# Embedding products computed between the routing steps, value projection by K halves, and the last two key blocks of the stick attention summed ahead

## The reference

```
# first block: two-level routing, then the experts
y = expert(hid)                      # hid = silu(x @ w_gate[e]) * (x @ w_up[e]); y = hid @ w_down[e]
# second block
u_x, u_g, q, k, v, g_lru, g_att = split(rmsnorm(x) @ w_in)
log_1m = where(causal, log_sigmoid(-z), 0)            # z = q k^T / 8, causal: key < query
suffix = cumsum(log_1m over keys, reversed) - log_1m
att    = where(causal, exp(log_sigmoid(z) + suffix), 0);   y_att = att @ v
...
x = x + sigmoid(rmsnorm(x) @ w_ple_gate) * (p @ w_ple)       # p: 512 x 256, w_ple: 256 x 1024
out = rmsnorm(x)
```

## Time and profile before

| | |
|---|---|
| median of 3 runs | 1800.84 us (1800.48 to 1802.74) |
| profiled execution | 1802.86 us, its span 1800.0 us |
| PE busy | 1711.8 us, 95% of the span |
| DVE, ACT, POOL busy | 696.6, 605.8, 567.0 us |
| mean granted clock of PE | 0.979 |
| stages of the span | routing 293 to 315, experts to 803, projections to 1042, stick attention to 1225, the rest to 1800 us |

### The profile page before, as it was taken

The page is one execution under the profiler, slowest core; times in us unless marked ns, Lnnn a source line. Parts: engine busy times, 40 slices in busy tenths (PEclk is TensorE's granted clock), DMA queues, the critical chain, the costliest instruction groups (busy, mean ns, idle before and its releaser), DMA issues.

```text
span 1800.0 us, 20351 instructions
## 1 busy us (share of the span) xinstructions
PE 1711.8 (95%) x8350; PEld 1195.8 (66%) x8350; DVE 696.6 (39%) x1060; ACT 605.8 (34%) x787; POOL 567.0 (32%) x263
## 2 busy tenths in 40 slices
PE   7989796999999999989999999999999999999995
PEld 5667574444444443447788977777777888888882
DVE  6564645233433333358541022223244322222325
ACT  5565444111000110025641255555233423232331
POOL 3232134222022201023434334443443444444440
PEclk9989998999999999999999999999999999999997
DMA  5121172699999999972221201112232222223101
GB/s 207 56 74 48 36 294 95 247 420 421 421 421 421 421 421 421 421 285 94 94 94 47 94 1 48 48 48 94 94 141 94 94 94 94 100 91 124 60 36 47
DMA packets 75068, 308.56 MB, mean 171 GB/s; under 512 B 3008, under 2 KB 4448, under 8 KB 50272
## 3 DMA queue, kind: packets, MB, share of 16 engines
q1 hardware_dynamic: 74704, 306.18, 43.6%
q0 software_dynamic: 272, 1.05, 0.2%
HBM read 305.12 MB, written 2.10 MB: 171 GB/s over the span
## 4 chain that ended last, share of the span: by engine, by line
PE 86%; DVE 7%; ACT 3%; issue 2%; POOL 1%; DMA 0%; DVEq 0%; SPq 0%; ACTq 0%
PE ps L857 42%; PE ps L1189 12%; PE ps L899 8%; PE ps L1213 6%; PE ps L1143 4%; PE ps L855 3%; PE ps L1336 2%; PE ps L1158 1%; ACT sb_slot L1403 1%; PE ps L1159 1%; PE ps L1321 1%; PE ps L1357 1%; PE ps L1306 1%; DVE sb_xT L2211 1%; ACT sb_F L1403 1%
## 5 line engine op out<-in xcount | busy, mean ns | idle before, releaser
L797 POOL TENSOR_TENSOR sb_w_parts<-sb_slot,sb_w_parts 128x2048 fp32r<-128x2048 f32 x59 | 274.9, 4660 | 381.6 <-ACT sb_w_parts L1403 381.6
L857 PE MATMUL ps<-sb_h_high,sb_w_parts 128*128 128x512 f32 x1120 | 269.4, 392 | 2.5 <-POOL sb_w_parts L797 2.5
L857 PEld LDWEIGHTS ps<-sb_h_high,sb_w_parts 128*128 128x128 f32 x1120 | 209.7, 188 | 51.0 <-POOL sb_w_parts L797 3.7
L1403 ACT ACTIVATE sb_w_parts<-sb_slot 128x2048 fp32r<-128x2048 f32 x59 | 112.7, 1912 | 186.7 <-PE ps L857 186.7
L1189 PE MATMUL ps<-sb_slot,sb_hT 128*64 128x512 f32 x768 | 171.1, 594 | 0.0
L857 PE MATMUL ps<-sb_hidden_high,sb_w_parts 128*128 128x512 f32 x704 | 165.2, 389 | 1.9 <-ACT sb_hidden_high L1403 1.9
L857 PEld LDWEIGHTS ps<-sb_hidden_high,sb_w_parts 128*128 128x128 f32 x704 | 132.1, 188 | 29.7 <-ACT sb_hidden_high L1403 2.3
L761 POOL TENSOR_TENSOR sb_tile_parts<-sb_slot,sb_tile_parts 128x1024 fp32r<-128x1024 f32 x32 | 79.7, 2492 | 202.5 <-ACT sb_tile_parts L1403 202.5
L857 PE MATMUL ps<-sb_h_low,sb_w_parts 128*128 128x512 f32 x560 | 138.0, 389 | 0.0
L1189 PEld LDWEIGHTS ps<-sb_slot,sb_hT 128*64 128x64 f32 x768 | 53.6, 137 | 106.2 <-issue 106.2
L857 PEld LDWEIGHTS ps<-sb_h_low,sb_w_parts 128*128 128x128 f32 x560 | 105.1, 188 | 21.8
(11 more groups left out here) (313 smaller groups left out, 2651.7 us busy)
## 6 DMA issues: line engine op xcount, KB each, us to landing
sb_slot<-w_up SPq DMA_DIRECT2D x24, 2048.0 KB, 15.5
sb_slot<-w_gate SPq DMA_DIRECT2D x24, 2048.0 KB, 15.4
sb_slot<-w_down SPq DMA_DIRECT2D x21, 2048.0 KB, 16.2
sb_slot<-w_in SPq DMA_DIRECT2D x14, 2048.0 KB, 7.9
sb_R<-w_down SPq DMA_DIRECT2D x11, 2048.0 KB, 16.0
sb_slot<-tiles SPq DMA_DIRECT2D x32, 512.0 KB, 3.4
sb_R<-w_gate SPq DMA_DIRECT2D x8, 2048.0 KB, 15.2
sb_R<-w_up SPq DMA_DIRECT2D x8, 2048.0 KB, 15.9
```

Source lines behind the costliest of these rows:

```text
L797: nc.gpsimd.tensor_tensor(low, raw_part(g), high.bitcast(F32), ALU.subtract).then_inc(w_low, 1)
L857: ins = nc.tensor.matmul(o, w[:, k, at:at + P], h[:, k, :], start=first, stop=last)
L1403: return nc.scalar.activation(dst, src, f, **kw)
```

## The change

1. `p @ w_ple` moves. Its operands (1.5 MB) are loaded in SP's list where chunk 6 was, into slot 2. PE makes `ple` 0 to 2 after the last `turn_h` and `ple` 3 to 7 after `rank`. ACT copies each result to a free piece of slot 2 or `hT`, SP stores the eight pieces (256 KB each) to a DRAM buffer, waits for all of them, and only then loads chunk 6. ACT waits for the same stores before the first expert's SiLU. SP reads the 2 MB back during the MLP.
2. The end. After each `pg` block a step `embed`: DVE multiplies the PSUM bank by `rstd`, ACT takes the sigmoid in the bank, DVE multiplies by `ple` in the bank and adds to x; ACT squares. The last sum of squares is two fp32 matmuls, one of `acc` with seven blocks and one of the eighth square, without DVE's last addition.
3. `v2` by K halves: an item holds 4 of the 8 K blocks and 512 columns. `vh` accumulates the first half in four banks, `v2` the second; 8 jobs, 192 matmuls of 512 columns in all.
4. Stick attention: DVE makes `Ltail` (key block 2, its second half with key block 3 added) and its high part, and signals `tail_done`; POOL waits for that instead of `sp_done` and makes one more low part. PE sums key blocks 2 and 3 for the query sums 0 and 1 together from `Ltail`; only two fp32 matmuls a head are left.

The job numbers shift: eight more before `ux`, eight fewer in `v2`, eight fewer at the end.

```diff
+    for n in range(3):
+        job("ple", n)
     step("route")
     job("rank")
+    for n in range(3, KD):
+        job("ple", n)
     step("place")
...
+            if base == "pg" and n:
+                for m in (0, 1) if n == 1 else (n,):
+                    if n > 1:
+                        step("embed", m)
+                    else:
+                        held.append(m)
...
     elif base == "v2":
-        ITEMS += [(base, (2 * n + h) * TT, TT) for h in range(2)]
+        ITEMS += [("vh", n * TT, TT), ("v2", n * TT, TT)]
...
-            chunk_load(6)
+            load(pT2, a["pT"].rearrange("(k p) n -> p k n", p=P), ld["p"])
+            for k in range(2):
+                load(w_ple[:, :, k, :], a["w_ple_2"][0, k * P:k * P + P, :].rearrange("p (n c) -> p n c", c=P), ld["p"])
             sp.wait_ge(w1_low, len(TILES1))
             chunk_load(1)
             finished(sp, ("tile", "out", KD - 1))
             chunk_load(0)
+            for n in range(KD):
+                taken(sp, ("ple", n))
+                load(ple_rows[n], ple_out[n], stored)
+            sp.wait_ge(stored, 16 * KD)
+            chunk_load(6)
...
-                            pool.wait_ge(sp_done, h + 1)
+                            pool.wait_ge(tail_done, h + 1)
...
+                            ins = nc.gpsimd.tensor_tensor(Ltail_low[h % 2], Ltail[h % 2], Ltail_high[h % 2].bitcast(F32), ALU.subtract)
...
+                if norm == 5:
+                    pe.wait_ge(acc_done, 7 * SQUARED.index(norm) + 6)
+                    nc.tensor.matmul(ps_[:, 7, :], C("ones"), acc, start=True, stop=False)
+                    pe.wait_ge(squared, 8 * SQUARED.index(norm) + KD)
+                    nc.tensor.matmul(ps_[:, 7, :], C("ones"), sq, start=False, stop=True).then_inc(summed, 1)
+                    return
...
                     def suffix_high(h):
                         pe.wait_ge(sp_done, h + 1)
-                        sums(h, tri_r, ones_r, Lhigh, (0, 1, 2))
-                        sums(h, C("negtri"), C("negones"), Lb, (3,))
+                        suffix(h, Lhigh)
+                        c, w_ = SEG[3]
+                        last = Lb[h % 2][:, c:c + w_]
+                        summed_keys(h, 3, 0, P, C("negtri"), last)
+                        summed_keys(h, 2, P, P, C("negones"), last)
+                        pe.wait_ge(tail_done, h + 1)
+                        for jt in range(2):
+                            summed_keys(h, jt, (2 - jt) * P, 2 * P, ones_r, Ltail_high[h % 2])
...
+                elif kind == "embed":
+                    n = arg[0]
+                    job = ("proj", "pg", n)
+                    finished(dve, job)
+                    v.tensor_tensor(bank(job), bank(job), rstd, ALU.mult).then_inc(pg_in, 1)
+                    if n:
+                        add_square(5, n - 1)
+                    else:
+                        dve.wait_ge(ld["p"], 64)
+                    dve.wait_ge(pg_done, n + 1)
+                    link(v.tensor_tensor(bank(job), bank(job), ple[:, n, :], ALU.mult))
+                    frees(v.tensor_tensor(xT[:, n, :], bank(job), xT[:, n, :], ALU.add), job)
+                    taken(dve, job)
+                    dve.sem_inc(x_new, 1)
...
+                        (c2, _), (c3, _) = SEG[2:4]
+                        v.tensor_copy(Ltail[h % 2][:, 0:P], Lb[h % 2][:, c2:c2 + P])
+                        link(v.tensor_tensor(Ltail[h % 2][:, P:2 * P], Lb[h % 2][:, c2 + P:c2 + 2 * P], Lb[h % 2][:, c3:c3 + P], ALU.add))
+                        v.tensor_copy(Ltail_high[h % 2], Ltail[h % 2]).then_inc(tail_done, 1)
```

More of the change, by code:

```diff
@@ L212, in plan @@
         weights_ahead(g)
+        if (base, first) == ("pg", 2):
+            for m in held:
+                step("embed", m)
         if base in ("ux", "ug") and first + (KD if base == "ug" else 0) in (6, 12):
@@ L249, in plan @@
                 step("feed", 5, n - 3 * KD)
-    for n in range(KD):
-        job("proj", "ple", n)
-        step("square", 5, n)
+            if base == "pg" and n:
+                for m in (0, 1) if n == 1 else (n,):
+                    if n > 1:
+                        step("embed", m)
+                    else:
+                        held.append(m)
     step("norm", 5)
@@ L310, in build @@
         xT_ = sb("xT", KD * S)
-        F = sb("F", 1024)
+        with ExitStack() as third:
+            F = third.enter_context(nc.sbuf_tensor("sb_F", [P, 1024], F32))
+        F_parts = sb("F_parts", 1024, F32R)
         cst = sb("cst", NCONST)
@@ L572, in weight_parts @@
             kind, i = buffer_of[g]
+            if ITEMS[g][0] in ("vh", "v2"):
+                return [view(WP, PAN * part + PAN // 2 * i, KD // 2, 512) for part in range(2)]
             return (WH[i], WL[i]) if kind == "whole" else tile_parts[i]
@@ L1126, in _, with ple_taken @@
                     x_bank, odd_bank, even_bank = (0, 1, 7, 2), (7, 0, 1, 4), (7, 0, 1, 2)
+                    def ple_taken(b):
+                        for n in range(KD):
+                            if J["ple", n] % JB == b:
+                                taken(pe, ("ple", n))
                     def gather(m, q):
@@ L1502, in _ @@
                     norm, n = arg
-                    if norm == 5:
-                        act.wait_ge(x_new, n + 1)
-                    else:
-                        taken(act, ("tile", "out", n))
-                        fn(hT[:, n, :], xT[:, n, :], ACT.Copy, scale=G("ffn_norm_g", n)).then_inc(xg_ready, 1)
+                    taken(act, ("tile", "out", n))
+                    fn(hT[:, n, :], xT[:, n, :], ACT.Copy, scale=G("ffn_norm_g", n)).then_inc(xg_ready, 1)
                     square(norm, n)
@@ L1557, in _ @@
                     job = st
-                    o = None if name in ("bl", "ba", "out2", "dn", "ple", "ux", "ug", "q2", "k2", "gl", "ga", "up", "pg") else bank(job)
+                    o = None if name in ("vh", "bl", "ba", "out2", "dn", "ux", "ug", "q2", "k2", "gl", "ga", "up", "pg") else bank(job)
                     if o is not None:
@@ L1576, in _ @@
                         fn(HC[c % 2][0][:, n % KD, :], relu[:, n % 2, :], ACT.Copy).then_inc(hid_high, 1)
-                    elif name == "pg":
-                        taken(act, job)
-                        fn(pgs[:, n, :], pgs[:, n, :], ACT.Sigmoid).then_inc(pg_done, 1)
+                elif kind == "embed":
+                    n = arg[0]
+                    job = ("proj", "pg", n)
+                    act.wait_ge(pg_in, n + 1)
+                    fn(bank(job), bank(job), ACT.Sigmoid).then_inc(pg_done, 1)
+                    act.wait_ge(x_new, n + 1)
+                    square(5, n)
                 elif kind == "soft":
@@ L1665, in _ @@
                     frees(fn(htok[:, t, cols], bank(st), ACT.Copy, scale=row_rstd[:, t:t + 1]), st)
+                elif kind == "ple":
+                    finished(act, st)
+                    frees(fn(ple_out[arg[0]], bank(st), ACT.Copy), st)
                 elif kind == "route":
@@ L1995, in _ @@
                                         ALU.subtract).then_inc(hid_low, 1)
-                    elif name == "ple":
-                        dve.wait_ge(pg_done, n + 1)
-                        finished(dve, st)
-                        if n:
-                            dve.wait_ge(x_new, n)
-                        frees(v.tensor_tensor(prod["ple"], bank(st), pgs[:, n, :], ALU.mult), st)
-                        taken(dve, st)
-                        v.tensor_tensor(xT[:, n, :], xT[:, n, :], prod["ple"], ALU.add).then_inc(x_new, 1)
                 elif kind == "headsum":
```

131 lines of the change are left out of this document (76 added, 55 removed).

## The result

The changed kernel takes 1773.14 us (median; 1772.05 to 1774.92) against 1801.61 us for the kernel before, timed beside it: ratio 0.9845, 95% interval 0.9833 to 0.9858. The forecast was 1774.0 us, within 1768.5 to 1781.5. The profiled execution took 1772.83 us with a span of 1771.0, 29.0 us less than the span before.

What follows compares the result with a forecast made beforehand. PE, busy 95% of the span, was taken as the bound, other engines counting only where PE waits. Terms -19.9 - 2.3 - 2.5 - 2.1 = -26.8 us from the 1800.84 median gave 1774.0 us, range 1768.5 to 1781.5.

Steps and rivals of the forecast that it cites:

- The end, -19.9: Behind the last gate product only block 7's round, square and table load remain, so the root starts 19.9 us earlier.
- the cover I named: At the end, even a half-clock second sum would end at 1767.7, before the table load allows the root at 1767.9.
- Routing, -2.3: Embedding products in PE's routing waits keep the clock up; the first gather falls from 10.18 to 7.85 us.
- rival b: Small parts pay in full and one clock dip elsewhere is gone: -4.4 - 1.7 on top, 1768 us; chance 0.13.
- v2, -2.5: Value projection: 192 matmuls of 512 columns take 43.6 us instead of 46.08 for 384 of 256.
- Stick, -2.1: Stick attention: seven pair periods each 0.65 us shorter, -4.5, against +2.4 in the first pair; bounds -6.5 to +3.
- The first pair: First pair of heads in stick attention: +1.6 us from later low parts and +0.8 from the clock, together +2.4.
- the 0.8 us that I gave to the clock: First pair of heads: with more PE idle time the already low clock may fall sooner, +0.8 us.
- Rival d: Expert stream starts late; each us chunk 6 is issued after about 324.7 costs one us: 1801 and more; chance 0.03.

Runs made afterwards that it cites:

- improved: Changed kernel with six unread matmuls in three PE idle times, POOL's first stick subtraction started earlier and the first pair's first fill low pass moved: 1772.08 us.
- gap_filled: Kernel before with only 16 unread matmuls added in routing, 6 ahead of the rank product and 10 behind it: 1799.45 us.
- stick_alone: Kernel before with only the stick attention part of the change: 1799.20 us against 1801.65 us.
- late_chunk: Changed kernel with one more wait in SP's list, so expert chunk 6 is issued only when the first chunk has been used: 1772.03 us.
- after_again: The changed kernel unchanged, timed once more: 1774.41 us.
- v2_alone: Kernel before with only the value projection by K halves: 1801.41 us against 1801.65 us.
- longer_rounds: Changed kernel with one more DVE multiplication by 1.0 in each round of embed: 1776.91 us (two executions).

## Why the prediction was right

- **The end, -19.9: -20.0.** Rounds of 2.92 us (I had 3.0), one block left. One term was wrong: the second sum, which I put at half of 1.02, is a whole fp32 product, 1.13 us. The clock was full, as I had said. It ended at 1758.76, 0.1 us ahead of the table load's end, so it cost nothing, but the cover I named was nearly used up; in `improved`, where it ran at a low clock (1.77 us), it was not enough.
- **Routing, -2.3: -2.27**, by the mechanism named (`gap_filled`), and 1.7 us more for the dip at 787, which I had only in rival b. Chunk 6 was issued at 315.34 (I said about 317), the next one near 328.5.
- **v2, -2.5: -2.34**; the passes themselves fell from 46.08 to 43.53 us, and 0.2 us came back in a longer eviction of 512 columns ahead of the scores.
- **Stick, -2.1.** The first pair lost 2.31 (+2.4) and the period fell by 0.75 to 0.77 us (0.65). The three DVE operations took 0.22, 0.28 and 0.29, POOL's 0.73, as priced. I had POOL 0.3 us late and PE waiting for it before the odd head's low sums; that wait isn't there. POOL ends at 1116.58 and PE's low sums begin at 1116.63 without a break, so the two tie, and the period fell by 0.1 us more than I wrote. `stick_alone` has the same: 20.76 and 21.38 us. Without the dip in the second pair of before the stage is 3.0 us shorter, against 2.1. The first pair was right in size, but for a reason of which I had only the half. The 1.5 us of added operations were priced; the 0.8 us that I gave to the clock were not lost to it (its dip there cost nothing), but to DVE and POOL in each other's way, 0.45 + 0.52 us on DVE's side. That 2.4 came out is luck to that extent.
- **Rival d** had a wrong rule, that each us of late stream costs one us. In `late_chunk` it cost 0.3 us where the rule gives 4 to 5, though the expert stage moved 421 GB/s and PE was busy in 99.7 of 100 us.
- **What the sum did not have**: dips. Before had 3, after 4, in other places; 1.7 us less at 787, 1.6 less in the second pair, 3.3 more behind the stick stage. They cancelled, and that is luck: any of them would have moved the total by as much as a whole small part of the change. The four terms themselves came to -27.7 us with the dips taken out, against -26.8. The other -1.2 us in the traces lies ahead of rank, where the trace of before has a dip at 40 us and that of after hasn't.

## What to carry to other kernels

An independent product of the right length is worth more in a wait of PE than its own time, where the clock falls behind the wait: moved there, the embedding products left the end 20.0 us shorter and gave 2.3 us in the gather besides, which unread products did too. Judge a small part by traces from a landmark behind the noisy start, and count the stretches of low clock before you say what a part is worth, but only those in which PE was the late one; by medians v2's 2.4 us were invisible. And before an engine is let start earlier, see which operations of the other come to lie under it.

## What the runs showed of the hardware that I had not expected

- Idle times of PE of about 1.9 and 2.5 us are followed by 3.4 us at 1.2 GHz in some kernels and by none in others, at the same place in the code; for one kernel the places repeated in a second trace (four of four in `after_again`). Two products of 0.88 us in each took away the three falls of after and the three of `v2_alone` there. What decides stays open.
- In all 14 traces the clock fell at about 787 us if, and only if, PE had been idle in routing at 300 us.
- A DVE cast of 0.29 us took 2.11 under a POOL subtraction, an addition with both inputs in SBUF 1.75 instead of 0.69 (in `longer_rounds`, under POOL's 4.56 us), ending 0.15 us after POOL in the first case and 0.55 in the second.
- The first 300 us differ by up to 3.4 us between executions; a dip at 40 us, there in eight of the 14 traces, parts them into two groups.
